# Opening transfers, and the order of gates, merges and output products at the end of the last mixer stage

## What is computed

```python
def reference(x, ...):
    for layer in range(2):                        # first_block
        u = rmsnorm(x, norm_mix[layer])
        x = x + (mlstm_mixer if layer == 0 else moba_mixer)(u, ...)      # stages A, B
        x = x + swiglu(rmsnorm(x, norm_ffn[layer]), ...)                 # F0, F1
    h = rms_norm(x, norm1_g)                      # second_block: stage C
    qa, ka, va, hy_in, qc, kc, vc, gate_logits = split(h @ w_in)
    out_a = window_attention(rope(qa), rope(ka), va, sink)               # 8 heads
    out_b = hyena_branch(hy_in, filters(filt_w1, filt_w2, filt_w3), ...)
    out_c = rms_norm(diff_attention(rope(qc), rope(kc), vc, lam), subln) # 4 heads
    g = sigmoid(gate_logits).reshape(S, 3, 1024)
    merged = g[:, 0] * (out_a @ w_oa) + g[:, 1] * (out_b @ w_ob) + g[:, 2] * (out_c @ w_oc)
    x = x + merged @ w_out
    return x + swiglu(rms_norm(x, norm2_g), ...)                         # F2
```

## Time and profile before

| | us |
|---|---|
| median of three runs | 1126.22 |
| lowest and highest | 1123.49, 1126.56 |
| profiled execution, as timed | 1125.78 |
| its span in the trace | 1124.0 |
| TensorE busy in it | 1073.8 |
| VectorE busy | 724.5 |
| ScalarE busy | 540.0 |

### The profile page before, as it was taken

How to read it: one execution, slowest core, us unless ns; L and a number is a source line. 1 busy time by engine, 2 the same in 40 slices (tenths; PEclk the granted TensorE clock), 3 DMA queues, 4 the chain that set the end, 5 groups by cost and what they waited for, 6 DMA issues and landing times.

```text
span 1124.0 us, 14634 instructions
## 1 busy us (share of the span) xinstructions
PE 1073.8 (96%) x4942; PEld 866.4 (77%) x4942; DVE 724.5 (64%) x1193; ACT 540.0 (48%) x828; POOL 59.5 (5%) x64
## 2 busy tenths in 40 slices
PE   4999999999999999999999999889799999999998
PEld 3777678888887778788888778767577877888887
DVE  2865775554557987755555577987848676555553
ACT  3564454444444556644344473645347535444442
POOL 5003000000000200000000000002400000000000
PEclk9999999999999999999999999999899999999999
DMA  9454256555555543566565543543244455555553
GB/s 250 125 169 131 77 164 190 187 186 187 188 186 172 169 147 127 158 190 189 184 191 188 176 150 113 169 132 113 76 133 135 144 169 169 187 187 187 187 187 112
DMA packets 133599, 182.04 MB, mean 162 GB/s; under 512 B 11446, under 2 KB 80322, under 8 KB 133490
## 3 DMA queue, kind: packets, MB, share of 16 engines
q1 hardware_dynamic: 132266, 178.40, 50.2%
q0 software_dynamic: 1056, 2.57, 1.1%
q10 hardware_dynamic: 232, 0.49, 0.1%
HBM read 180.36 MB, written 1.05 MB: 161 GB/s over the span
## 4 chain that ended last, share of the span: by engine, by line
PE 77%; DVE 13%; ACT 5%; issue 2%; DMA 2%; SPq 1%; POOL 0%; DVEq 0%; ACTq 0%; POOLq 0%
PE ps L1793 15%; PE ps L1804 14%; PE ps L1796 14%; PE ps L1814 7%; PE ps L1815 6%; PE ps L1819 6%; DVE wlo L1032 4%; PE ps L1778 2%; PE ps L1780 2%; PE ps L1779 2%; ACT whi L571 1%; PE ps L1884 1%; DMA raw<-in_a_w_in 1%; PE ps L1867 1%; PE ps L2006 1%
## 5 line engine op out<-in xcount | busy, mean ns | idle before, releaser
L1032 DVE TENSOR_TENSOR wlo<-raw,whi 128x1024 fp32r<-128x1024 f32 x338 | 407.1, 1236 | 151.8 <-ACT whi L571 151.3
L571 ACT ACTIVATE whi<-raw 128x1024 fp32r<-128x1024 f32 x338 | 342.3, 1052 | 117.3 <-DMA raw<-in_ffn_w_out 29.0
L1793 PE MATMUL ps<-whi,ath 128*128 128x512 f32 (+1 forms) x896 | 360.6, 403 | 9.1 <-DVE atl L1046 5.5
L1796 PE MATMUL ps<-whi,atl 128*128 128x512 f32 (+1 forms) x896 | 351.9, 393 | 0.0
L1804 PE MATMUL ps<-wlo,ath 128*128 128x512 f32 (+1 forms) x896 | 240.7, 390 | 3.3 <-DVE wlo L1032 3.3
L1793 PEld LDWEIGHTS ps<-whi,ath 128*128 128x128 f32 x896 | 170.4, 190 | 53.7 <-issue 11.6
L1804 PEld LDWEIGHTS ps<-wlo,ath 128*128 128x128 f32 x896 | 167.2, 188 | 40.1 <-DVE wlo L1032 5.4
L1796 PEld LDWEIGHTS ps<-whi,atl 128*128 128x128 f32 x896 | 170.7, 191 | 33.5 <-issue 0.5
L1814 PE MATMUL ps<-whi,brh 128*128 128x512 f32 x272 | 106.5, 392 | 0.5 <-issue 0.5
L1815 PE MATMUL ps<-whi,brl 128*128 128x512 f32 x272 | 105.9, 389 | 0.0
L1108 DVE TENSOR_TENSOR brl<-ps,brh 128x512 fp32r<-128x512 f32 x33 | 22.8, 692 | 95.2 <-ACT brh L617 95.2
(11 more groups left out here) (339 smaller groups left out, 1027.2 us busy)
## 6 DMA issues: line engine op xcount, KB each, us to landing
raw<-in_ffn_w_in SPq DMA_DIRECT2D x176, 256.0 KB, 2.9
raw<-in_ffn_w SPq DMA_DIRECT2D x132, 256.0 KB, 2.9
raw<-in_w_in SPq DMA_DIRECT2D x104, 256.0 KB, 2.9
raw<-in_ffn_w_out SPq DMA_DIRECT2D x88, 256.0 KB, 2.8
raw<-in_a_w_in SPq DMA_DIRECT2D x48, 256.0 KB, 3.3
raw<-in_b_w_in SPq DMA_DIRECT2D x48, 256.0 KB, 3.0
raw<-in_a_w_out SPq DMA_DIRECT2D x16, 256.0 KB, 2.8
raw<-in_b_w_out SPq DMA_DIRECT2D x16, 256.0 KB, 2.8
```

Source lines behind the costliest of these rows:

```text
L571: a_(unit_view(whi, slot, w), unit_view(raw, slot, w), ACT.Copy).then_inc(hi_ready, 1)
L1032: v_.tensor_tensor(unit_view(wlo, slot, w), unit_view(raw, slot, w), unit_view(whi, slot, w), ALU.subtract).then_inc(lo_ready, 1)
L1793: mm(ps[bk + t][:, 0:w], ath[:, k, t * P:(t + 1) * P], rh[:, kk, :], start=k == 0, stop=False)
L1796: mm(ps[bk + t][:, 0:w], atl[:, k, t * P:(t + 1) * P], rh[:, kk, :], start=False, stop=False)
```

## The change

Two places of the program are changed.

In the **opening**, the tokens are SyncE's first transfers, and the four units of input block 0 come next, ahead of the nine small rows. The identity and the first gain row go through ScalarE. The other constants are issued by ScalarE only after it has split unit 0. GpSimd issues filter weights 1 and 2 first, then waits until unit 0 has landed before it issues the rest. TensorE makes five products on a tile of zeros before anything has landed, into a bank that nobody reads, then turns the tokens tile by tile, each as it lands. ScalarE and VectorE make the halves of the first pair before they split unit 0, and the other three pairs after. The transpose of the other gain rows stands behind block 0, and the first filter product in the middle of block 1.

The diff (two hunks that only renumber waits on `cleared` are left out):

```diff
@@ -352,23 +352,9 @@
         def _(sp):
-            nc.sync.dma_start(con[:, 0:P], D["consts"][:, 0:P]).then_inc(sem("ident_loaded"), 16)
             xv = D["x"][0].rearrange("(t p) n -> p t n", p=P)
-            sp.wait_ge(sem("cleared"), 1)
-            mix = D["norm_mix"].rearrange("l (k p) -> (l k) p", p=P)
-            nc.sync.dma_start(grow[0:mix.shape[0], :], mix).then_inc(sem("mix_loaded"), 16)
             for t in range(NT):
                 nc.sync.dma_start(x[:, t, :], xv[:, t, :]).then_inc(sem(f"x_loaded{t}"), 16)
-            rows = [("ffn", D["norm_ffn"].rearrange("l (k p) -> (l k) p", p=P), P),
...
-            for name, src, w in rows:
-                r = GROWS[name]
-                nc.sync.dma_start(grow[r:r + src.shape[0], 0:w], src).then_inc(sem("grow_loaded"), 16)
@@ -422,7 +408,20 @@
-            for i in range(6):
+            load_in(U_A, D["a_w_in"][0], 0)
+            sp.wait_ge(sem("cleared"), 2)
+            rows = [("ffn", D["norm_ffn"].rearrange("l (k p) -> (l k) p", p=P), P),
...
+            for name, src, w in rows:
+                r = GROWS[name]
+                nc.sync.dma_start(grow[r:r + src.shape[0], 0:w], src).then_inc(sem("grow_loaded"), 16)
+            for i in range(1, 6):
                 load_in(U_A + 4 * i, D["a_w_in"][0], 512 * i)
@@ -455,6 +454,9 @@
         def _(pool):
+            nc.gpsimd.dma_start(fw12[0:33, 0, :], D["filt_w1_2"][0]).then_inc(sem("filt_loaded"), 16)
+            nc.gpsimd.dma_start(fw12[:, 1, :], D["filt_w2_2"][0]).then_inc(sem("filt_loaded"), 16)
+            pool.wait_ge(raw_loaded[0], 32)
             nc.gpsimd.dma_start(wg[:, :, :], D["a_w_in"][0].rearrange("(k p) n -> p k n", p=P)[:, :, 3072:3080])\
@@ -464,8 +466,6 @@
             nc.gpsimd.dma_start(work[0:64, 18968:18968 + 2048], D["filt_w3_2"][0]).then_inc(sem("filt_loaded"), 16)
-            nc.gpsimd.dma_start(fw12[0:33, 0, :], D["filt_w1_2"][0]).then_inc(sem("filt_loaded"), 16)
-            nc.gpsimd.dma_start(fw12[:, 1, :], D["filt_w2_2"][0]).then_inc(sem("filt_loaded"), 16)
             nc.gpsimd.dma_start(posi[:, :], D["positions"][0].rearrange("(t p) -> p t", p=P), allow_slow_non_contiguous=True)\
@@ -556,8 +556,10 @@
-            nc.scalar.dma_start(con[:, P:N_FIRST], D["consts"][:, P:N_FIRST]).then_inc(sem("con1_loaded"), 16)
-            act.wait_ge(sem("cleared"), 1)
+            nc.scalar.dma_start(con[:, 0:P], D["consts"][:, 0:P]).then_inc(sem("ident_loaded"), 16)
+            act.wait_ge(sem("cleared"), 2)
+            mix = D["norm_mix"].rearrange("l (k p) -> (l k) p", p=P)
+            nc.scalar.dma_start(grow[0:mix.shape[0], :], mix).then_inc(sem("mix_loaded"), 16)
             for name, src in (("w", D["conv_w_2"][0].rearrange("j (m p) -> (j m) p", p=P)),
@@ -652,14 +654,19 @@
             act.wait_ge(sem("gcol_ready"), 1)
+            def mix_gain(f):
+                return gcol[:, GROWS["mix"] + f:GROWS["mix"] + f + 1]
+            turn_hi(0, mix_gain, (0,))
             feed(1)
-            turn_hi(0, lambda f: gcol[:, GROWS["mix"] + f:GROWS["mix"] + f + 1])
-            act.wait_ge(sem("cols_turned"), 2)
-            a_(gcol[:, 16:P], ps[7][:, 272:384], ACT.Copy).then_inc(sem("gcol_ready"), 1)
+            nc.scalar.dma_start(con[:, P:N_FIRST], D["consts"][:, P:N_FIRST]).then_inc(sem("con1_loaded"), 16)
+            turn_hi(0, mix_gain, (1, 2, 3))
             feed(3 + AHEAD)
...
             evac(0, lambda t: A_qk[:, t, 0:512])
+            act.wait_ge(sem("cols_turned"), 2)
+            a_(gcol[:, 16:P], ps[7][:, 272:384], ACT.Copy).then_inc(sem("gcol_ready"), 1)
             act.wait_ge(sem("f_arg"), 1)
@@ -963,10 +970,10 @@
-            def d_exp(h):
+            def d_exp(h, comps=(0, 1)):
                 act.wait_ge(sem("d_max"), h + 1)
                 c = sm[:, 208 + 32 * (h % 2):]
-                for comp in range(2):
+                for comp in comps:
                     for t in range(NT):
@@ -990,17 +997,20 @@
                 feed(D_STEPS[min(i, CH)])
-                if 0 < i < CH:
+                if i in (1, 3):
                     d_exp(i)
                 if i == 2:
+                    d_exp(i, (0,))
                     act.wait_ge(sem("merged"), 4)
                     gate_evac(24, 0)
+                    d_exp(i, (1,))
                 if 0 <= i - 1 < CH:
...
             gate_evac(25, 1)
-            feed(U_OC + 2)
+            feed(U_OC + 3)
             act.wait_ge(sem("sub_ready"), 1)
@@ -1138,11 +1148,13 @@
+            v_.memset(hid[:, 0, :], 0.0).then_inc(sem("cleared"), 1)
             v_.memset(grow[:, :], 0.0).then_inc(sem("cleared"), 1)
...
             v_.memset(A_o[:, :, :, ADV:ADV + 1], 0.0).then_inc(sem("cleared"), 1)
+            turn_lo(0, lambda f: gcol[:, GROWS["mix"] + f:GROWS["mix"] + f + 1], (0,))
             feed(1)
-            turn_lo(0, lambda f: gcol[:, GROWS["mix"] + f:GROWS["mix"] + f + 1])
+            turn_lo(0, lambda f: gcol[:, GROWS["mix"] + f:GROWS["mix"] + f + 1], (1, 2, 3))
             feed(3 + AHEAD)
@@ -1156,6 +1168,7 @@
                 dve.wait_ge(sem("f_mm"), i + 1)
+                dve.wait_ge(sem("gcol_ready"), 2)
                 b, f = GROWS["b1"] + 2 * i, GROWS["f1"] + 2 * i
@@ -1732,8 +1745,9 @@
             d_prob(0)
+            feed(U_GC + 2)
+            merge(0, DOWN_BANKS, U_GC)
             feed(D_STEPS[0])
-            merge(0, DOWN_BANKS, U_GC)
             for i in range(1, CH + 1):
@@ -1757,8 +1771,8 @@
             merge(1, OB_BANKS, U_OC)
+            merge(2, BR_BANKS, U_W, (0,))
             feed(U_W + 2)
-            merge(2, BR_BANKS, U_W, (0,))
             turn_lo(6, lambda f: 0.5, (0, 1))
@@ -1937,26 +1951,28 @@
+            pe.wait_ge(sem("cleared"), 1)
+            for _ in range(5):
+                mm(ps[7][:, 0:S], hid[:, 0, 0:P], hid[:, 0, :], start=True, stop=True)
             pe.wait_ge(sem("ident_loaded"), 16)
             pe.wait_ge(sem("mix_loaded"), 16)
...
-            def x_first(p):
-                if p == 0:
-                    for t in range(NT):
-                        pe.wait_ge(sem(f"x_loaded{t}"), 16)
-            turn(lambda t: x[:, t, :], x_first)
+            for t in range(NT):
+                pe.wait_ge(sem(f"x_loaded{t}"), 16)
+                for p in range(4):
+                    for f in range(2):
+                        c = (2 * p + f) * P
+                        ins = nc.tensor.transpose(ps[TBANKS[p]][:, f * S + t * P:f * S + (t + 1) * P],
+                                                  x[:, t, c:c + P], ident)
+                    if t == NT - 1:
+                        ins.then_inc(turned, 1)
+            units(0, use=0)
             pe.wait_ge(sem("grow_loaded"), 16 * (len(GROWS) - 1))
...
             nc.tensor.transpose(ps[7][:, 256:384], grow[:, :], ident).then_inc(sem("cols_turned"), 1)
-            units(0, use=0)
-            pe.wait_ge(sem("con1_loaded"), 16)
-            pe.wait_ge(sem("filt_loaded"), 48)
-            mm(ps[7][0:64, 0:S], fw12[0:33, 0, :], con[0:33, CONSTS["zT"][0]:CONSTS["zT"][0] + S],
-               start=True, stop=True).then_inc(sem("f_mm"), 1)
             def gate_products(k, t, part):
@@ -1966,7 +1982,13 @@
             pe.wait_ge(sem("wg_split"), 2)
-            units(1, beside=gate_products)
+            units(1, 0, 2, beside=gate_products)
+            pe.wait_ge(sem("gcol_ready"), 2)
+            pe.wait_ge(sem("con1_loaded"), 16)
+            pe.wait_ge(sem("filt_loaded"), 48)
+            mm(ps[7][0:64, 0:S], fw12[0:33, 0, :], con[0:33, CONSTS["zT"][0]:CONSTS["zT"][0] + S],
+               start=True, stop=True).then_inc(sem("f_mm"), 1)
+            units(1, 2, 4, beside=gate_products)
@@ -2416,12 +2438,15 @@
                         d_scores(h + 2)
+                if h == CH:
+                    pe.wait_ge(sem("h_lo"), 1)
+                    pe.wait_ge(sem("d_exp"), 4 * CH)
+                    down_unit(U_OB % RING, 0, True, False, U_OB + 1, obh, obl, OB_BANKS)
                 if h >= 1:
                     d_pv(h - 1)
-            pe.wait_ge(sem("h_lo"), 1)
-            pe.wait_ge(sem("d_exp"), 4 * CH)
-            for k in range(3):
-                down_unit((U_OB + k) % RING, k, k == 0, False, U_OB + k + 1, obh, obl, OB_BANKS)
+            for k in (1, 2):
+                down_unit((U_OB + k) % RING, k, False, False, U_OB + k + 1, obh, obl, OB_BANKS)
             for p in range(2):
@@ -2441,15 +2466,14 @@
-            down_end([(U_OC + k, k, k == 0, k == 3) for k in range(4)], (brh, brl), BR_BANKS, (3, 0),
+            down_end([(U_OC + k, k, k == 0, k == 3) for k in range(4)], (brh, brl), BR_BANKS, (2, 1),
                      lambda: mg_turn((0, 1)))
-            pe.wait_ge(turned_lo, 8 * 6 + 2)
-            down_unit(U_W % RING, 0, True, False, U_W + 1, ath, atl, W_BANKS)
-            mg_turn((2, 3))
-            for k in range(1, 6):
-                if k in (2, 4):
+            for k in range(6):
+                if k == 2:
+                    mg_turn((2, 3))
```

(3 more changed lines are left out.)

14 lines of the change are left out of this document (7 added, 7 removed).

## The result

| | before | after |
|---|---|---|
| median, us (6 runs each) | 1125.76 | 1118.44 |
| lowest to highest | 1122.40 to 1127.64 | 1116.19 to 1120.74 |
| profiled execution, as timed | 1125.78 | 1116.19 |
| its span | 1124.0 | 1114.5 |
| TensorE busy in it | 1073.8 | 1081.9 |

The ratio is 0.9937, 95% interval 0.9916 to 0.9957: 7 us faster, where 15.2 were forecast, and the median lies above the range. The sign was right, the size half. The first thing to see is that TensorE is now busy 8.1 us longer. The five products on zeros (ten instructions in the trace) are 4.6 of these; its other work has not grown, so it did part of that at its lower clock.

The account below looks back on a forecast made before the run. TensorE, busy 96% of the span, was taken as the bound, so only its idle or slow-clock times could pay. 1125.8 us less 10.5 (opening) and 4.7 (stage C) gave 1110.6, range 1105.5 to about 1116.

Parts of the forecast that it names:

- The opening up to the end of block 0: Opening: block 0 ends at 21.7 us, where the filter product started at 32.43 before; 10.5 us gained.
- Turn: Opening, TensorE: the first pair of token tiles is turned at 7.8 us, with ends of 6.9 and 11.6.
- wait before unit 1: Opening, block 0: TensorE stands still 1.0 us until ScalarE has split unit 1.
- The first rival: Opening: tokens or units 1 to 3 land 2 to 4 us late, 1112.6 to 1114.6; chance 0.18.
- "I take 0" for the filter product: Middle of block 1: filter weights 3 at 30.4 against a product at 30.2, so no wait counted.
- The clock: Rival, between the turns and unit 0: TensorE's clock at half or falling back, 1112.0 to 1113.5; chance 0.08.
- the fourth rival: Filter product in block 1: filter weights 3 late, each microsecond past 30.2 costs one, up to 1129.2; chance 0.02.
- Nothing for VectorE's filter argument: Block 1: the argument comes 2.5 us later against TensorE, at most 0.3 us shows, put at nothing.
- Stage C: End of stage C: five TensorE waits, 6.1 us in all, shrink by 4.7 us, with ends of 2.5 and 6.1.
- The evacuation's wait: Stage C, third head: gate evacuation behind two exponentials, not four; 1.1 of the 1.75 us wait goes.
- the one before branch C: Stage C, third branch's products: late low halves give a new 0.4 us wait, net gain 0.65 us.
- the merged tiles' turn: Stage C, second merge ahead of two splits: 0.3 of the 2.22 us wait stays, 1.9 goes.

Follow-up runs that it names:

- the first experiment: The changed kernel with ScalarE copying the other gain columns behind the split of unit 5, not behind those of units 6 and 7: 1114.70 us, ratio 0.9902.

## Why the prediction was wrong

**The opening up to the end of block 0: right, a little too careful.** Turn at 7.9 (forecast 7.8), first large product at 9.30 (9.8), wait before unit 1 of 0.17 (1.0), end of block 0 at 20.7 (21.7). The first rival, late landings, did not touch tokens or units 0 to 3.

**"I take 0" for the filter product: the step that failed.** I costed it by one of its inputs, filter weights 3, at 30.4 against 30.2. By that input I was nearly right (GpSimd had them at 29.50, and they let the product go at 29.99 in the first experiment). The diff adds a second wait, on `gcol_ready`, and moves ScalarE's copy behind `feed(8)` and the evacuation of block 0, that is behind the landing of unit 7. I even named the parameter columns among what the filter product needs, and put no time on them. I listed what stood behind the new waits on GpSimd and SyncE and not what the moved copy now stands behind on ScalarE. Its price was 2.4 to 3.9 us. The landing of unit 7 at 29.8 was not costed either: I said that unit 4 is needed at 22.0 and stopped there, though the same 1 MB from GpSimd that I timed shares the DMA engines with units 6 and 7.

**The clock: right rival, wrong place and size.** I priced a clock that falls between the turns and unit 0 at 1.4 to 2.9 us and took 2.22 us of idling without a fall as evidence against. That was the luck of one trace: in three of five the same wait was followed by the half clock. It fell at the filter product, and what it costs depends on what follows: 7 us in block 1 behind 2.44 us of idling, since it stays at half as long as gate products stand beside the large ones. My chance of 0.08 was for the wrong place; the fourth rival had the right place with the wrong input and needed 15 us of lateness to cost 15, where 2.4 us cost 10.

**Nothing for VectorE's filter argument.** It did no harm in the changed kernel, because the slow block hid it, but as soon as block 1 ran at full clock GpSimd's sums beside it cost 4.07 us of waiting and the clock again. GpSimd's transfer was moved by 6 us, and its sums moved with it, from 24.45, where they lay beside unit splits, to beside the argument. I followed the transfers of GpSimd and not its arithmetic.

**Stage C: right by its waits, too low by its time.** 4.7 forecast, 5.1 by the waits, 7.4 measured. The 2.4 us that the clock cost behind two of the old waits were put at nothing. The evacuation's wait has 0.66 left (0.65 forecast), the one before branch C 0.30 (0.4), and the merged tiles' turn none (0.3 forecast).

**The sum.** The opening was forecast at 10.5 us and gave none that shows (ratio 0.9997, between 2.6 us faster and 1.9 slower). Stage C was forecast at 4.7 and gave 7.4. So the failed step took all of the opening's gain, and it was luck that stage C covered a part of the loss, which left 7.3 of the 15.2. At the product near 105 us the opening still seems to give 2.0 (106.8 against 104.8 in the mean of three traces each), but these scatter by 3 us. With the two late steps put right the kernel is 15.8 us below before. By difference that is 8.4 for the opening and 7.4 for stage C, so that it comes near the forecast 15.2 with both terms off in opposite directions. Up to block 0's end and at 105 us (10.45) the opening's terms were sound; what is lost behind that was not followed in full.

## What to carry to other kernels

When an edit makes an instruction wait for one more thing, price that thing where its producer now stands in its own engine's order, with every landing ahead of it, and do the same for arithmetic that waits for a moved transfer. A wait on TensorE is not worth its length alone: look at what it runs next, since 2.4 us ahead of a stretch mixed with very small products cost 10 us here, and 2.2 us ahead of transposes and plain products cost 2.2 in two traces and 3.9 in three. One trace without a fall of the clock is no evidence that a wait is safe: look at a second trace, or at the granted clock of every run. A gain that moves a whole stage earlier is safe only if the transfers of the next stage come earlier too.
